# Three weight tiles instead of two inside the join of a two-layer fp32 block

## What is computed

```python
for l in range(DEPTH_2):                      # two layers
    hin = _rms_norm(x, norm_mix_pre[l])
    proj = hin @ w_in[l]
    ...                                       # four mixers
    x = x + _rms_norm(mixed, norm_mix_post[l])
    hin = _rms_norm(x, norm_mlp_pre[l])
    u = hin @ mlp_w_up[l]
    ...                                       # convolution over tokens, gate
    x = x + _rms_norm(y, norm_mlp_post[l])
```

## Time and profile before

| | |
|---|---|
| median of three runs | 4159.36 us (4152.49 to 4159.55) |
| profiled execution | 4161.6 us, its span 4159.8 us |
| TensorE busy | 3780.5 us, 91% |
| VectorE busy | 2547.5 us, 61% |
| ScalarE busy | 1674.5 us, 40% |
| GpSimd busy | 355.8 us, 9% |
| loads moved | 619.59 MB, mean 149 GB/s |

### The profile page before, as it was taken

The page is one execution under the profiler, slowest core; times in us unless marked ns, Lnnn a source line. Parts: engine busy times, 40 slices in busy tenths (PEclk is TensorE's granted clock), DMA queues, the critical chain, the costliest instruction groups (busy, mean ns, idle before and its releaser), DMA issues. The chain is left out here.

```text
span 4159.8 us, 60383 instructions
## 1 busy us (share of the span) xinstructions
PE 3780.5 (91%) x24414; PEld 3407.3 (82%) x24414; DVE 2547.5 (61%) x3571; ACT 1674.5 (40%) x2121; POOL 355.8 (9%) x354
## 2 busy tenths in 40 slices
PE   6783468899999998999999999999999999999997
PEld 6751148799999997889988888888989978888886
DVE  4438864554555555655587576766555577567675
ACT  3220023443333334444465454544344455454452
POOL 1006740100000002100010000001100010000001
PEclk9856689999999999999999999999999999999999
DMA  4300013344445453533444554544443435454553
GB/s 153 121 21 0 0 41 131 122 176 177 172 180 182 171 189 132 186 134 128 165 152 172 192 186 170 191 173 146 177 159 132 153 137 187 179 188 178 195 180 127
DMA packets 90024, 619.59 MB, mean 149 GB/s; under 512 B 9936, under 2 KB 12496, under 8 KB 26192
## 3 DMA queue, kind: packets, MB, share of 16 engines
q1 hardware_dynamic: 89808, 616.59, 40.9%
HBM read 614.45 MB, written 2.10 MB: 148 GB/s over the span
## 5 line engine op out<-in xcount | busy, mean ns | idle before, releaser
L1929 DVE TENSOR_TENSOR wlo<-raw,whi 128x2048 fp32r<-128x2048 f32 (+3 forms) x422 | 924.3, 2190 | 313.9 <-ACT whi L1752 310.6
L1486 PE MATMUL gemm<-x_pair,whi 128*128 128x512 f32 x2816 | 996.5, 398 | 18.2 <-DVE x_pair L2094 14.5
L1752 ACT CAST whi<-raw 128x2048 fp32r<-128x2048 f32 (+3 forms) x422 | 767.1, 1820 | 282.8 <-DMA raw<-in_stream_dram 279.2
L1487 PE MATMUL gemm<-x_pair,wlo 128*128 128x256 f32 x2816 | 790.0, 281 | 0.0
L1486 PEld LDWEIGHTS gemm<-x_pair,whi 128*128 128x128 f32 x2816 | 529.9, 188 | 146.4 <-issue 10.9
L316 ACT CAST whi<-raw 128x2048 fp32r<-128x2048 f32 x176 | 335.3, 1908 | 592.2 <-DMA raw<-in_stream_dram 547.2
L1487 PEld LDWEIGHTS gemm<-x_pair,wlo 128*128 128x128 f32 x2816 | 533.3, 189 | 0.7
L1486 PE MATMUL gemm<-f_pair,whi 128*128 128x512 f32 x1408 | 509.6, 405 | 20.8 <-DVE wlo L1929 20.8
L329 PE MATMUL gemm<-xh,whi 128*128 128x272 f32 x1616 | 470.5, 291 | 43.0 <-DVE wlo L321 21.6
L331 PE MATMUL gemm<-xh,wlo 128*128 128x272 f32 x1616 | 469.2, 290 | 0.0
L330 PE MATMUL gemm<-xl,whi 128*128 128x272 f32 x1616 | 467.3, 289 | 0.0
(11 more groups left out here) (404 smaller groups left out, 6554.9 us busy)
## 6 DMA issues: line engine op xcount, KB each, us to landing
raw<-in_stream_dram SPq DMA_DIRECT2D x494, 1024.0 KB, 4.8
raw<-in_stream_dram SPq DMA_DIRECT2D x64, 896.0 KB, 4.5
raw<-in_stream_dram SPq DMA_DIRECT2D x32, 768.0 KB, 4.2
raw<-in_stream_dram SPq DMA_DIRECT2D x4, 952.0 KB, 4.6
xT<-in_hT_dram SPq DMA_DIRECT2D x1, 2176.0 KB, 9.0
out_dram<-xT SPq DMA_DIRECT2D x4, 512.0 KB, 2.8
const<-in_const_dram SPq DMA_DIRECT2D x1, 1504.0 KB, 8.5
b_raw<-in_s_dram SPq DMA_DIRECT2D x1, 1024.0 KB, 5.1
```

What stands on the lines that cost most here:

```text
L1486: pe.matmul(both, whi[:, slot(n), k * P:k * P + P], pairs[:, :, c, :], start=(k == 0), stop=False, skip_group_check=True)
L1487: return pe.matmul(bank(use)[:, 0:T2], wlo[:, slot(n), k * P:k * P + P], pairs[:, 0, c, :], start=False, stop=(k == nk - 1), skip_group_ch ...
L1752: act.copy(whi[:, slot(n), 0:wide], raw[:, slot(n), 0:wide]).then_inc(w_hi, 1)
L1929: dve.tensor_tensor(wlo[:, slot(n), 0:wide], raw[:, slot(n), 0:wide], whi[:, slot(n), 0:wide].bitcast(F32), ALU.subtract).then_inc(w_lo, 1)
```

## The change

TensorE runs the matmuls of the first **three** tiles for each chunk; the wait for each tile's split and bank now stands at its own first matmul. Behind the join it skips three tiles instead of two. The split of the third tile moves to the beginning: ScalarE casts it before the first chunk of the new state (`c in (0, 10)`, and 2 + 0 // 10 is again the third tile), VectorE subtracts ahead of the scaled chunk c=2. On ScalarE and VectorE the place of the fifth tile's split is what it was (behind the first two tiles' work). The loads and GpSimd are as before.

```diff
                     def join(e):
                         n = FIRST2[e]
                         use = USE2[PLAN2[n][:2]]
-                        for i in range(2):
-                            pe.wait_ge(w_lo, n0 + n + i + 1)
-                            pe.wait_ge(bank_free, u0 + use + i - 3)
                         for c in range(DC):
                             pe.wait_ge(x_low, DC * e + c + 1)
-                            for i in range(2):
+                            for i in range(3):
+                                if c == 0:
+                                    pe.wait_ge(w_lo, n0 + n + i + 1)
+                                    pe.wait_ge(bank_free, u0 + use + i - 3)
                                 if e == 0:
                                     out, at = bank(use + i)[:, 0:T2], slice(c * P, (c + 1) * P)
                                     pe.matmul(out, whi[:, slot(n + i), at], xh2[:, c, :], start=(c == 0), stop=False)
@@ TensorE, the loop over tiles
-                        if n in FIRST2 or n - 1 in FIRST2:
+                        if any(n - i in FIRST2 for i in range(3)):
                             continue
@@ ScalarE, join
                         for c in range(DC):
-                            if c in (5, 10):
+                            if c in (0, 10):
                                 hi(FIRST2[e] + 2 + c // 10)
@@ VectorE, join
                         for c in range(DC):
+                            if c == 2:
+                                lo(FIRST2[e] + 2)
                             if DC * e + c >= 4:
                                 dve.wait_ge(joined, DC * e + c - 3)
                             dve.scalar_tensor_tensor(out=scaled_y[:, c % 4, :], in0=y2[:, c, :], scalar=gain(post, c), in1=rstd_y[:, :],
                                                      op0=ALU.mult, op1=ALU.mult).then_inc(scaled, 1)
-                            if c == 9:
-                                lo(FIRST2[e] + 2)
```

## The result

The changed kernel takes 4175.19 us in the median of seven runs (4169.73 to 4182.41), the kernel before 4159.36 (4152.49 to 4171.78): the ratio is 1.0038, 95% interval 1.0027 to 1.0049, so 11 to 20 us slower. The profiled executions are 20.8 us apart (spans 4180.6 and 4159.8). The forecast was 4175 us.

A forecast was written before the change was run, and what follows sets the result against it. TensorE, busy 91% of the span, bounds the kernel. Joins to fifth tile +2.4 (A, C) and +8.8 (B, D), clock +4.2: 15.4 us slower, 4177.0 profiled, less 2.2 for the median: 4175 us; range 4163 to 4185.

The forecast's parts named there:

- TensorE sets the pace of a three-tile join: In all four joins: chunks become 1.51 or 1.47 us on TensorE, longer than the 1.27 us in which they arrive.
- A: A join at the head of a layer, first matmul to new norm's root: forecast 28.7 us, 5.7 longer.
- B: A join ahead of the MLP, first matmul to new norm's root: forecast 28.0 us, 5.0 longer.
- The start is 1.9 us later: At each join's beginning: VectorE's early subtraction delays the first matmul by 1.9 us, bounds 0 and 2.8.
- Length of the joins: First matmul to new norm's root: start 1.9, chunks 24.2 or 23.5, clock 2.3, end 0.3; 28.7 or 28.0 us.
- C: The other join at the head of a layer: forecast 28.7 us, 5.7 longer.
- D: The other join ahead of the MLP: forecast 28.0 us, 3.8 longer.
- the slow start: At each join's start TensorE's clock is at its lower level: 2.3 us each, now all on the path.
- The fifth tile in A and C, 7.4 us behind the root: Behind these joins: its split is ready 7.4 us after the root, TensorE waits 1.3 us more; +1.2 us each.
- the rival of shared engines: Behind the joins: three loads share engines and end together, 14 us more, 4189 us; chance 0.06.
- The fifth tile in B and D, 13.0 us behind the root: Behind these joins: ScalarE's and VectorE's chain keeps its start at 13.0 us, idle grows to 7.4; together +8.8 us.
- The clock behind the fifth tile: After the 7.4 us idles in B and D the clock falls: 2.1 us each, +4.2; in A and C 0.

## Why the prediction was right

The forecast of 4175 us stands beside 4175.19. The mechanism was right: TensorE sets the pace of the longer joins, and the fifth tile's split holds TensorE behind them. That the numbers agree to 0.2 us is luck: in the traces three terms were off, they sum to 18.5 us instead of 15.4, and the medians happen to lie closer together than the traces.

- **TensorE sets the pace of a three-tile join.** Right. The distance of the sums in A after is 1.51 us (forecast 1.51) in one chunk, 1.50 in the mean, and 1.48 in B (forecast 1.47), and TensorE is busy in the whole window. Two rows of A's chunks in TensorE's timeline after:

```profile
1597.87 0.60 PE L1482 MATMUL att<-sq,const 128*128 128x256 f32 x2
...
1599.38 0.59 PE L1482 MATMUL att<-sq,const 128*128 128x256 f32 x2
```

- **The start is 1.9 us later.** It was 2.17 us (7.25 us of idle ahead of B instead of 5.08). VectorE's subtraction took 2.81 us, not 2.28, beside GpSimd's first two additions, which took 3.62 us together (0.89 and 2.77). VectorE's and GpSimd's timelines of join A after:

```profile
1585.16 2.81 DVE L1929 TENSOR_TENSOR wlo<-raw,whi 128x2048 fp32r<-128x2048 f32 x1
```

```profile
1584.93 3.62 POOL L1459 TENSOR_TENSOR xT<-xT,y_scaled 128x256 f32<-128x256 f32 x2 [17.66 <-DVE y_scaled L2110]
```

The prediction had counted the contention on GpSimd's side alone, as in the earlier trace rows, where the subtraction began 0.16 us ahead of the addition beside it and took its usual 2.28 us. Here it began 0.23 us behind the first addition, and took 0.5 us more in each of the four joins.

- **Length of the joins.** 28.7 us forecast for A and C, start included: 26.18 + 2.17 = 28.4 and 28.2 measured. 28.0 for B and D: 28.7 and 28.5, because the start came 0.3 us later than forecast and the slow start cost (1 - 0.90) x 26.5 = 2.7 us there and not 2.3.
- **The fifth tile in A and C, 7.4 us behind the root.** 7.56 and 7.57, after an idle of 1.32 us (forecast 1.3). The three loads went one behind the other; the rival of shared engines did not come.
- **The fifth tile in B and D, 13.0 us behind the root.** 13.01 in both, after 7.50 us (forecast 7.4). The moved subtraction and the early split of the fifth tile showed what holds it: ScalarE's and VectorE's queue behind the root.
- **The clock behind the fifth tile.** In B and D I took 2.1 us each and it was 1.8 and 1.6. In A and C I took 0 and it was 1.7 each. That is the step that failed: I judged the 1.3 us by a hole of 2.11 us that had done no harm in one trace. Holes like it did lower the clock in other executions, and the turn of the norm ahead of this idle was left out of the argument. The bound of 1.7 us that I kept for the range was the value. The three products behind the turn showed that the idle does it.
- **Sum.** Joins +11.2 forecast, +11.7 measured; clock +4.2 forecast, +6.8 measured; together 15.4 against 18.5 in the traces. The medians are 15.8 us apart. The gap of 2.7 us is inside the interval. An estimate accounts for part of it: with two tiles the clock fell behind the fifth tile of B and D in four of eight cases, at 1.7 us each, but in neither of the two in the trace of the kernel before, which takes about 1.7 us off the 18.5. The rest is open.

The Trainium skill's sentence on loop structure (TensorE: Matmul & The Clock Gate, Loop structure matters more than you think), that matmuls behind a long wait run cold, agrees: 0.79 us for the first 512-column matmul behind 7.50 us of waiting, 0.50 us and a grant of 1.00 when the wait is filled. The Trainium skill's advice on the same page (What's actually happening), that the ramp is under 1% of a typical span and that no count of cold matmuls is to be fitted, would have left 6.8 of 18.5 us out. The 1% is not contradicted by that: 6.8 us is 0.2% of this span.

## What to carry to other kernels

Before moving work into an idle stretch, look at what comes after it: if the next tile's preparation starts at the end of the stretch, each tile taken out from behind it only uncovers that preparation. Ask which engine sets the pace of the stretch, since a cost there (a slow start, an added tile) is hidden while another engine leads and counts once the lead changes. Move the preparation first: here the kernel with its splits moved was 4 to 12 us faster, by the traces almost all of it from the one moved ahead of the join, and moving the work itself cost 11 to 20. And follow a gain past the first tile: 1.7 us at the fifth tile were 0.5 at the sixth.

## What the runs showed of the hardware

- A short idle can lower TensorE's clock: 1.2 to 1.4 us behind four tiny matmuls of 0.60 us gave 0.83 over the next ten us in 13 of 13 cases (and 2.2 us in the one other), and three products in between kept 1.00 in both. Idles of 1.2 to 2.2 us between dense matmuls did it in 6 of 16, and not in the same ones from one execution to the next (2.11 us in A without a fall, 2.20 us in D with one).
- VectorE's subtraction of 128x2048 with two SBUF inputs took 2.28 us alone, 2.28 us when an addition of GpSimd's began 0.16 us behind it (the addition then took 2.70 us instead of 0.91), and 2.81 us when it began 0.23 us behind an addition. In these rows the one that began later is the one that took longer.
- Three loads of 1 MB issued within 0.85 us reached ScalarE's casts 2.5 us apart in C; ScalarE's timeline of the kernel after, behind join C (start, length, engine, line, operation, in brackets the idle before it and what ended it):

```profile
2912.62 1.91 ACT L1752 CAST whi<-raw 128x2048 fp32r<-128x2048 f32 x1 [2.81 <-DMA raw<-in_stream_dram]
2915.11 1.90 ACT L1752 CAST whi<-raw 128x2048 fp32r<-128x2048 f32 x1 [0.58 <-DMA raw<-in_stream_dram]
2917.57 1.90 ACT L1752 CAST whi<-raw 128x2048 fp32r<-128x2048 f32 x1 [0.57 <-DMA raw<-in_stream_dram]
```

In A the first two casts stood 2.48 us apart, and the third came 3.9 us behind the second, after an idle of 2.03 us. Why it differs is open.
